# An encoder layer in one launch: local keys turned in the projection, loads placed ahead of their stages, and the second exponential of global attention written to SBUF

## The reference

```python
h = rmsnorm(x, g_pre_mix)
qa, ka, va, qb, kb, vb = split(h @ w_in)         # 1536 columns: 8+2+2 heads global, 8+2+2 heads local, 64 wide
A = softmax(rope(rmsnorm(qa)) @ rope(rmsnorm(ka)).T * 64**-0.5) @ va        # all 2048 keys, 4 query heads to a key head
B = softmax over 384 keys around each block of 128 queries, plus a bias by distance and a sink logit per head
x = x + rmsnorm(concat(A, B) @ w_o, g_post_mix)
u = relu(rmsnorm(x, g_pre_ffn) @ w_ffn_up)
x = x + rmsnorm((u * u) @ w_ffn_down, g_post_ffn)
```

## Time and profile before

| | us |
|---|---|
| median of 3 runs | 2894.25 (2889.93 to 2895.68) |
| the profiled execution | 2890.22 |
| its span, first to last instruction | 2888.6 |
| PE busy | 2705.4 (94%) |
| DVE busy | 1827.9 (63%) |
| ACT busy | 1429.2 (49%) |
| POOL busy | 803.3 (28%) |

### The profile page before, as it was taken

One profiled execution on the slowest core, in us unless ns is written; L12 is line 12 of the kernel. 1 busy time (PEld: TensorE's weight loads), 2 busy tenths in 40 slices (PEclk: granted clock), 3 DMA queues, 4 the chain that ended last, 5 costly groups with the idle time before them and its releaser, 6 DMA issues. The chain is left out here.

```text
span 2888.6 us, 36041 instructions
## 1 busy us (share of the span) xinstructions
PE 2705.4 (94%) x12274; PEld 2185.6 (76%) x12274; DVE 1827.9 (63%) x2503; ACT 1429.2 (49%) x2122; POOL 803.3 (28%) x603
## 2 busy tenths in 40 slices
PE   7999599999999978988995999999998999999998
PEld 5888467777777747976874888788886888888887
DVE  5666499999999947865556666675653343343433
ACT  3222177777777747973334544554443333233332
POOL 1111178888888854541110000000000000000000
PEclk9999799999999989998997999999999999999999
DMA  5333421111111122327876333533325445355442
GB/s 181 107 108 102 122 67 30 31 34 28 35 30 32 23 75 70 84 67 218 207 202 216 124 117 97 209 107 100 114 92 189 171 172 182 121 196 179 172 172 98
DMA packets 295611, 338.16 MB, mean 117 GB/s; under 512 B 73059, under 2 KB 219635, under 8 KB 293292
## 3 DMA queue, kind: packets, MB, share of 16 engines
q1 hardware_dynamic: 269980, 317.92, 35.7%
q10 hardware_dynamic: 23552, 13.64, 1.5%
q0 software_dynamic: 1936, 4.74, 0.6%
HBM read 234.10 MB, written 97.86 MB: 115 GB/s over the span
## 5 line engine op out<-in xcount | busy, mean ns | idle before, releaser
L126 PE MATMUL d_pr<-d_w_hi,d_s_hi 128*128 128x512 f32 x1024 | 399.7, 390 | 11.6 <-DVE d_s_lo L1872 11.6
L1871 DVE TENSOR_TENSOR d_w_lo<-d_w_raw,d_w_hi 128x1024 fp32r<-128x1024 f32 x128 | 156.8, 1225 | 386.2 <-ACT d_s_hi L1848 382.3
L127 PE MATMUL d_pr<-d_w_lo,d_s_hi 128*128 128x512 f32 x1024 | 399.5, 390 | 0.0
L128 PE MATMUL d_pr<-d_w_hi,d_s_lo 128*128 128x512 f32 x1024 | 399.3, 390 | 0.0
L644 POOL TENSOR_TENSOR p_sum<-p_sum,p_hi 128x1024 f32<-128x1024 f32 x160 | 383.3, 2396 | 37.0 <-issue 19.7
L126 PE MATMUL u_pr<-u_t_hi,u_w_hi 128*128 128x512 f32 x896 | 351.2, 392 | 32.3 <-DVE u_t_lo L1687 31.9
L127 PE MATMUL u_pr<-u_t_lo,u_w_hi 128*128 128x512 f32 x896 | 350.1, 391 | 0.0
L128 PE MATMUL u_pr<-u_t_hi,u_w_lo 128*128 128x512 f32 x896 | 350.1, 391 | 0.0
L676 ACT ACTIVATE p_hi<-s_ps 128x1024 fp32r<-128x1024 f32 x256 | 263.3, 1028 | 157.0 <-PE s_ps L767 155.7
L720 DVE TENSOR_TENSOR p_lo<-s_ps,p_hi 128x1024 fp32r<-128x1024 f32 x256 | 312.5, 1221 | 29.5 <-ACT s_ps L677 22.3
L704 DVE TENSOR_REDUCE part_max<-m_ps 128x1 f32<-128x1024 f32 x251 | 304.6, 1214 | 33.1 <-PE m_ps L749 32.9
(11 more groups left out here) (219 smaller groups left out, 5384.5 us busy)
## 6 DMA issues: line engine op xcount, KB each, us to landing
d_w_raw<-in_w_ffn_down SPq DMA_DIRECT2D x128, 512.0 KB, 3.8
u_w_raw<-in_w_ffn_up SPq DMA_DIRECT2D x32, 1024.0 KB, 6.0
act_blocks<-u_s_out SPq DMA_DIRECT2D x128, 256.0 KB, 6.2
d_s_lo<-act_blocks SPq DMA_DIRECT2D x128, 256.0 KB, 2.7
u_t_lo<-h_blocks SPq DMA_DIRECT2D x14, 1024.0 KB, 10.9
x_in<-in_x SPq DMA_DIRECT2D x16, 512.0 KB, 4.3
q_split<-q_out ACTq DMA_DIRECT2D x16, 512.0 KB, 3.3
q_turned<-w_raw SPq DMA_DIRECT2D x16, 512.0 KB, 3.4
```

The lines of the kernel that those rows point to most:

```text
L126: nc.tensor.matmul(out, stat_hi, mov_hi, start=first, stop=False)
L127: nc.tensor.matmul(out, stat_hi, mov_lo, start=False, stop=False)
L128: return nc.tensor.matmul(out, stat_lo, mov_hi, start=False, stop=last)
L1871: nc.vector.tensor_tensor(w_lo[:, n % SLOTS], w_raw[:, n % RAW], w_hi[:, n % SLOTS].bitcast(F32), ALU.subtract)
```

## The change

It does several things at once, on all engines:

- **project** turns the local q and k heads too: ten more transpositions a tile, one more copy by ACT, and stores of the turned heads in place of two stores of unturned ones.
- **attend_global** loads keys in halves, makes the row of the bias and has it spread in DRAM, loads the local keys and the first local queries in its last 16 iterations, and keeps the maxima positive (a plane of the keys is -1 in place of 1, so `neg_max` goes). And the second exponential goes to `p_all`, a tile in SBUF with two slots, not back into its banks: `low` reads it there, PE's next scores wait for ACT's second exponential and no more for `low`, and ACT's second exponential waits for the `low` two units before.
- **attend_window** turns no keys and no queries; it loads the bias with one row shifted per partition, uses three banks for scores, and orders PE's work otherwise. It also loads w_o and the first tiles for stage 4. Loops are written out.
- **mix_heads** finds these in SBUF; the scaling of the global output moves from POOL to a matmul that spreads `rden` and a DVE multiply, the loads of a tile move from SP's queue to ACT's; half of the blocks for `ffn_up` stay in SBUF.
- **ffn_up** starts with these blocks and its first weights in SBUF. The arithmetic of stages 5 and 6 is as before.

```diff
@@ project
-            def keep_turned(t, s, p):
-                act.wait_ge(qk_turned, t + 1)
-                at_least(act, qk_stored[s], 32 * p)
-                nc.scalar.activation(qk_t[:, s], qk_ps[:, 0:10], ACT.Copy).then_inc(qk_kept, 1)
+            def keep_turned(t, s, p, b):
+                act.wait_ge(qk_turned, place(t, b) + 1)
+                at_least(act, qk_stored[s], 64 * p)
+                nc.scalar.activation((qk_t, qkb_t)[b][:, s], qk_ps[:, 0:10], ACT.Copy).then_inc(qk_kept, 1)
...
                 if not known(t, NT - 1):
                     turn(t + 1, 1 - s)
+                if not (isinstance(t, int) and t < 2):
+                    turn_qk(t - 2, s, 1)
                 chunk(t, s, 1)
                 chunk(t, s, 2)
-                turn_qk(t - 1, 1 - s)
+                turn_qk(t - 1, 1 - s, 0)
@@ attend_global
+        p_all = scratch["up_first"][:].rearrange("p (s k) c -> p s (k c)", s=2)
...
                 nc.scalar.activation(p_hi[:, slot], scored, ACT.Exp).then_inc(p_hi_ready, 1)
-                nc.scalar.activation(scored, scored, ACT.Exp).then_inc(probs_ready, 1)
+                at_least(act, p_lo_ready, at - 1)
+                nc.scalar.activation(p_all[:, u % 2], scored, ACT.Exp).then_inc(probs_ready, 1)
...
                 if m == PAIRS - 1:
                     nc.vector.drain()
-                    nc.vector.tensor_reduce(row_max[:], part_max[:], AX, ALU.max)
-                    nc.vector.drain()
                     at_least(dve, max_placed[n % 2], 16 * QT * (n // 2))
-                    nc.vector.tensor_scalar(neg_max[:, n % 2], row_max[:], -1.0, None, ALU.mult).then_inc(max_ready, 1)
+                    nc.vector.tensor_reduce(row_max[:, n % 2], part_max[:, n % 2], AX, ALU.max).then_inc(max_ready, 1)
...
-                dve.wait_ge(p_hi_ready, at + 1)
                 dve.wait_ge(probs_ready, at + 1)
                 at_least(dve, low_used, at - SLOTS + 1)
-                nc.vector.tensor_tensor(p_lo[:, slot], scored, p_hi[:, slot].bitcast(F32), ALU.subtract).then_inc(p_lo_ready, 1)
+                nc.vector.tensor_tensor(p_lo[:, slot], p_all[:, u % 2], p_hi[:, slot].bitcast(F32), ALU.subtract).then_inc(p_lo_ready, 1)
...
-                at_least(pe, p_lo_ready, at - 1)
+                at_least(pe, probs_ready, at - 1)
@@ attend_window
+            for g in range(NG):
+                heads = slice(GRP * g, GRP * (g + 1))
+                sp.dma_start(bias[:, heads], bias_tiles[:, heads]).then_inc(bias_in[g], 16)
...
+                if 8 <= n < 8 + KT:
+                    sp.dma_start(scratch["w_o_raw"][:, n - 8], w_o_tiles[n - 8]).then_inc(ahead_loaded, 16)
...
                 for h in range(GRP):
-                    if not known(n, TOTAL - 1):
+                    turn_probs(n, s, h)
+                if not known(n, TOTAL - 1):
+                    for h in range(SB, GRP):
                         scores(n + 1, 1 - s, b + s, h)
-                    if h == 0 and not known(n, TOTAL - 2):
-                        turn_q(n + 2, s, b + 1)
-                    if h:
-                        turn_probs(n, s, h - 1)
-                turn_probs(n, s, GRP - 1)
@@ mix_heads
+            def load_heads(t, s):
+                at_least(act, heads_turned, t - 1)
+                act.dma_start(heads[:, s], scratch["mix"][t]).then_inc(heads_loaded[s], 16)
+                at_least(act, ht_lo_made, t - 1)
+                sum_and_scale_loads(act, scratch, t, s, sums_loaded[s])
...
                 square(t, s, 1)
+                if not known(t, NT - 2):
+                    load_heads(t + 2, s)
...
+            def scale_heads(t, s):
+                dve.wait_ge(scaled, t + 1)
+                nc.vector.tensor_tensor(sums[:, s], sums[:, s], scale[:], ALU.mult).then_inc(hn_made, 1)
@@ ffn_up
-            load_w(0)
-            for o in range(7):
-                load_t(0, o)
-                if o == 2:
-                    load_w(1)
+            load_w(1)
```

More of the change, by code:

```diff
@@ L82, in every @@
         body(t, t % 2, t // 2)
[L85 to L100, removed]
 def heads_view(ap, h):
@@ L919, in step @@
+                sp.dma_start(scratch["mix"][b][:, cols], o[:, g].rearrange("p h c -> p (h c)")).then_inc(stored[g], 16)
             def step(n, g, b):
-                if not known(n, TOTAL - 2):
-                    load_q(b + 1, g)
+                if n > 0 and n + 3 < TOTAL:
+                    load_q(n + 3)
+                if n == 6:
+                    sp.wait_ge(den_inverted, 1)
+                    for part, tile in enumerate((rden_hi, rden_lo)):
+                        sp.dma_start(scratch["rden"][part].rearrange("h (t q) -> (h t) q", q=P), tile[:].bitcast(F32)).then_inc(rden_stored, 16)
@@ L983, in _ @@
                 load_v(0, g)
-            pool.wait_ge(const_in, 80)
+            nc.gpsimd.memset(scratch["rd"][:].bitcast(F32), 0.0)
+            nc.gpsimd.memset(scratch["pick"][:].bitcast(F32), 0.0)
+            pool.drain()
+            for part in range(2):
+                for e in range(2):
+                    row = 2 * HD * part // 2 + 32 * e
+                    last = nc.gpsimd.memset(scratch["pick"][row:row + 1, e * HD:(e + 1) * HD].bitcast(F32), 1.0)
+                    if part == 1 and e == 1:
+                        last.then_inc(rd_filled, 1)
+                    pool.drain()
             gap(0, 0)
@@ L1948, in build @@
         "act": dram("act_blocks", [4, FC, P, NB]),
     }
-    for n, stage in enumerate((project, attend_global, attend_window, mix_heads, ffn_up, ffn_down)):
-        if n < upto:
-            stage(nc, a, scratch) if n < 5 else stage(nc, a, scratch, out)
+    with ExitStack() as whole:
+        sb, _, _ = make_alloc(nc, whole)
+        scratch["ident"] = sb("ident", [P, P])
+        scratch["sink"] = sb("sink", [P, 8])
+        project(nc, a, scratch)
+        with ExitStack() as through:
+            sb, _, _ = make_alloc(nc, through)
+            scratch["t_first"] = sb("u_t_lo", [P, 7, KT // 2, NB], F32R)
+            scratch["up_first"] = sb("u_w_first", [P, KT, 2 * P])
+            shared = scratch["t_first"][:].rearrange("p o k n -> p (o k n)")
+            keys, queries = 4 * (SEQ + 2 * P), 4 * GRP * P
+            scratch["wkt"] = shared[:, 0:keys].rearrange("p (g e n) -> p g e n", g=NG, e=2)
+            scratch["wq_all"] = shared[:, keys:keys + queries].rearrange("p (s n) -> p s n", s=4)
+            scratch["wq_one"] = shared[:, keys + queries:keys + 2 * queries].rearrange("p (s n) -> p s n", s=4)
+            attend_global(nc, a, scratch)
+            with ExitStack() as ahead:
+                sb, _, _ = make_alloc(nc, ahead)
+                scratch["w_o_raw"] = sb("wo_raw", [P, KT, D])
+                scratch["heads"] = sb("m_heads", [P, 2, D // 2])
+                scratch["sums"] = sb("m_sums", [P, 2, KT // 2, P])
+                scratch["rd"] = sb("m_rd", [P, 2, KT // 2, P], F32R)
+                scratch["pick"] = sb("m_pick", [P, P], F32R)
+                attend_window(nc, a, scratch)
+                mix_heads(nc, a, scratch)
+            ffn_up(nc, a, scratch)
+        ffn_down(nc, a, scratch, out)
```

528 lines of the change are left out of this document (243 added, 285 removed).

## The result

The change makes the kernel slower: 3031.87 us in the median of 4 runs (3030.09 to 3036.04), against 2892.37 before (2889.93 to 2895.68, 4 runs). The ratio is 1.0484, 95% interval 1.0465 to 1.0502. The forecast was 3004 in a range of 2950 to 3065.

A forecast was written before the change was run, and what follows sets the result against it. DVE and POOL taking turns were to bound the global loop: +163 there, +12.5 projection, -60 window attention, 0 mixing, -5.5 ffn_up, +110 on 2890.2, giving 3000; 4 added made 3004 us, range 2950 to 3065.

The forecast's parts named there:

- The turns: Global loop: `low` and POOL's operations, both on SBUF, never overlap; 26.3 us an iteration, +5.1 each, +163 us in all.
- The path to PE: Global loop: the delay reaches PE through `p_hi` slots, ACT's second exponential and late maxima; some 5 us of waiting an iteration.
- `low` keeps 1.22 us beside POOL's adds: Global loop, sign in the changed profile: if `low` keeps this time there, the prediction is wrong.
- The sum of one `low` and one add close to the distance between them: Global loop, sign in the changed profile: both durations, near 2 and near 3 us, add up to about their distance.
- This is all that moving the second exponential can give: 38 us: Global loop: about 1.2 us of an iteration is waiting, scores for `low`; 32 x 1.2 = 38 us at most.
- `neg_max` ... nothing: Global loop: removing `neg_max` saves DVE about 1.6 us an iteration, but was given no gain because DVE has slack.
- rival A: Global loop: `low` meets POOL between its reads, no turns; PE's 20.0 us an iteration, 38 us gained, 2803 us; chance 0.07.
- Window attention: Window stage: -30 at the start, 4 more off before the loop, -26 in the loop; -60 us in sum.
- DVE's own work bounds: Window loop: the ring through DVE's bias operations opens, leaving DVE's work; 5.05 us an iteration from 5.88, -26 us.
- Projection: Projection stage: ten more transpositions a tile cost +16, an earlier copy at the end takes 3.5 off; +12.5 us.
- ffn_up: Start of this stage: blocks and weights already in SBUF bring the first product earlier; -5.5 us (-3 to -8).
- Mixing: Mixing stage: earlier start -13, sixteen more matmuls +3.7, waits for loads issued by ACT +10; together 0 us (-15 to +25).

The follow-up runs named there:

- Experiments 1: Changed kernel with the second exponential back in its PSUM banks, `low` reading it there and PE's scores waiting for `low`: 2844.02 us, ratio 0.9836.
- experiment 2: Kernel before with only the second exponential moved to its own SBUF tile, PE's scores waiting for ACT's exponential only: 3051.06 us, ratio 1.0555.
- experiment 4: Changed kernel with BY_ADDS 5 in place of 7, so POOL adds four units an iteration in place of six: 2962.02 us, ratio 1.0247.
- experiment 6: Changed kernel with each of POOL's six adds an iteration replaced by two memsets, the short additions kept: 2852.97 us, ratio 0.987.
- experiment 5: Kernel before with only `neg_max` removed, maxima placed as they are and the row of ones made -1: 2861.21 us, ratio 0.9904.
- Experiments 3: Changed kernel with the 2 MB bias copy cut into 8 parts of 256 KB in iterations 2 to 9: 2998.67 us, ratio 1.0377.
- 7: Changed kernel with the whole bias copy in iteration 4 in place of 2, away from the second group's keys and values: 3022.46 us.
- 8: Changed kernel with the same bias copy in iteration 2, issued by ACT on its own queue: 3022.70 us.
- 9: Changed kernel with the bias row written once to DRAM in iteration 2, then spread DRAM to DRAM in iteration 3: 2999.55 us.
- experiment 12: Changed kernel with the second exponential in PSUM, bias copy in 8 parts, and window attention's values load issued by SP, not POOL: 2797.53 us, ratio 0.9676.
- 11: Changed kernel with the second exponential in PSUM, bias copy in 8 parts, and four `w_rden` buffers in window attention, not two: 2810.30 us.

## Why the prediction was right, and where it was not

**The turns: right in mechanism and in size.** The forecast was 26.3 us an iteration and +163; the loop has 26.0 in the mean of 30 iterations, +157.5, and +5.8 in the first iteration (68.05 us from the stage's start to the first `p_sum`, against 60.0, of which 2.3 are that the first scores start 28.5 us into it and not 26.2). Experiments 1 and 2 show that the tile in SBUF alone does it, 4 and 6 that it is the meeting with POOL's reads: `low` is not slow by itself, and memsets do not hold it up. The path to PE was named in part: the late maxima were (60.0 us), and that POOL must free the slots of `p_hi`; that PE's scores would wait for the second exponential was wrong, no such wait shows; that ACT's copy of the output stands behind that wait, and costs PE 67.6 us, was not. The shares of a meeting were as taken from the earlier trace rows: 1.08 and 2.26 us. What failed is how I got from there to the iteration. I summed DVE's and POOL's work over an iteration and added 0.7 us; experiment 4 shows that it goes unit by unit, and there the same sum (21.1 + 0.7 = 21.8) missed the 24.07 by 2.3 us. With six adds in eight units the two ways give nearly the same number (six turns of 3.34, one unit of 2.8 and one of 2.32 are 25.2, and the product that adds POOL's sum is 0.9 more), which is why 26.3 came out: for the iteration, that was in part luck.

**Signs.** `low`'s median was 1.50 us, not near 2 (its mean is 1.75), and the adds 3.17, near 3 as said. By the recorded sign "`low` keeps 1.22 us beside POOL's adds" experiment 2, with a median of 1.24, would have spoken against the turns that cost it 160 us. PE was to wait some 5 us an iteration for ACT's second exponential or DVE's maxima; it waited 4.1 (127.6 in 31), for the maxima and for ACT's copy of the output. "The sum of one `low` and one add close to the distance between them" was wrong: 2.26 + 3.16 is far over 3.34, since each duration contains the wait for the other. The work of both without the waits, 1.08 + 2.26, is what fills the distance.

**"This is all that moving the second exponential can give: 38 us" and "`neg_max` ... nothing": both wrong, though neither changed the sum, since the turns cover both.** The 1.2 us that PE waited for `low` were not the shared banks. `neg_max` took 1.58 us of DVE's row because it too waited in POOL's adds, though only one operand that it reads lies in SBUF; the `low` behind it came late, and the profile names `low`. Without it PE waits for `low` 2.1 us in the whole loop (experiment 5), so moving the exponential could give 0.25 us an iteration (20.25 less the 20.0 that I counted for PE), not 1.2; experiment 6, with its short turns left in, did not gain even that. I had the rows of the cause in hand, and gave it nothing since "DVE has slack": slack in the mean, not in the unit where the wait falls. Of rival A's 38 us in the loop, had there been no turns, 28 would have come from `neg_max`.

**The term that was missing: +26 us in one iteration.** I looked at SP's extra loads in the last 16 iterations and gave them nothing, which held. I did not cost the copy of the bias row in iteration 2 at all. It is the largest part of what the forecast missed by, 26.3 of 29.7 us; the other misses, 10 us too much off in window attention and 7.5 too little in mixing among them, nearly cancel, which is luck. Experiments 3, 7, 8 and 9 give its cause in steps: the copy and not the keys beside it; not SP's queue, since ACT's did the same; its source, since from DRAM it hides.

**Window attention: -50 for -60.** The start gave 37.5 us where I had 34 (the first bias operation 5.1 us into the stage, forecast 6). The loop fell to 5.47 us an iteration, (1437.4 - 1267.7) / 31, and not 5.05. The step that failed is "DVE's own work bounds": POOL, which is 60% busy (96.3 of 160 us), held ACT's exponentials up, by the load it issues and the 1.8 us behind it. With the load on SP the loop goes at 5.09 us (experiment 12); the buffer was not it (11). That POOL's row alone bounds the loop is not shown: it counts 5.2 us an iteration, and the loop takes 5.5.

**Projection, +11.5 for +12.5**, and **ffn_up, -5.9 for -5.5**: as worked out. **Mixing, -7.5 for 0**: the start gave 14 us (13), the end is as before, and from first to last product the 16 tiles take 193.2 us against 186.6, +6.7, of which 3.7 are the extra matmuls as counted. So the waits for the loads that ACT issues cost some 3 us, not 10; the profile shows PE waiting for `m_rd` 5.4 us in 5 times. The loads landed sooner than I had counted: in the middle of the stage (1500 to 1650 us after, 1360 to 1500 before) `m_heads` takes 2.8 us in the median from issue to landing, against 7.1.

## What to carry to other kernels

An operand's place is part of the cost of an instruction on DVE wherever POOL reads SBUF beside it: look at what POOL reads at that time before a PSUM operand is moved to SBUF, and look for small DVE instructions that take ten times their own length, since these are the same wait already in the kernel. Ask of a wait that the profile names what stood ahead of the instruction that it names; taking away that one, four elements wide, was worth 28 us here, and the big move it seemed to call for cost 160 and gained nothing in any run. Go through every transfer that a change adds, its source too, above all one that is issued once.

## What the runs showed of the hardware

- DVE with two operands in SBUF and POOL reading SBUF exclude each other for the whole instruction: a turn of `low` and an add takes 3.34 us, 1.08 and 2.25 us of work. With POOL only writing (memset) they do not (1.21 to 1.23 us in 131 meetings). The Trainium skill ("SBUF — State Buffer", section "Who interferes with whom") says both, and that a reduction never takes part: here it keeps 1.21 us inside an add, and the four-element reduction that replaced `neg_max` takes 0.16 us where `neg_max`, a multiplication by -1 from SBUF to SBUF, took 1.58. So an instruction of DVE that reads only one operand from SBUF can take part too.
- With a 2 MB copy in 2 KB rows out of 8 partitions of SBUF the DMA engines moved 60 GB/s at a 0.48 busy share, and the transfers beside it took up to 27 us each to be issued for some 45 us, whichever engine's queue the copy was in; out of DRAM they moved 179 GB/s at 0.54, and the load behind took 3.5 us. The busy share is the same, so it is not that fewer engines work: each packet takes 3.5 times as long (298 ns, 84 ns). Why it does stays open.
- A DMA issued by POOL cost it not only 0.84 us but, two instructions later, 1.8 us more of a wait that the profile gives to nothing (36.0 in 20 times); it was nearly gone when SP issued the load. The code has a POOL drain at that place; by which way the one causes the other was not tried.
